# Compressing cached tokens: 32x32 blocks turned on VectorE, pages fetched over every second partition, direct products

## The chip, the cores and the metric

One NeuronCore of a Trainium2 chip runs the whole program once. The metric is the device time of that execution in microseconds. Everything is fp32.

## The reference, cut to what matters

The program is a four-layer decoder trunk that serves one prompt of 256 tokens and 8 sample sequences, each with 1024 cached tokens. Layers 0 and 3 use native sparse attention. One part of it compresses keys and values: each run of 32 tokens, taken every 16 tokens, is turned by a small two-layer network into one key and one value for each of the 4 KV heads.

```python
def _nsa_compress(kv_pad, cmp_pos, w1, w2):
    b, tpad = kv_pad.shape[:2]
    n_chunks = tpad // CMP_STRIDE                       # 64 for a sample, 16 for the prompt
    chunks = kv_pad[:, :, :2].reshape(b, n_chunks, CMP_STRIDE, 2, NSA_KV_HEADS, NSA_HEAD_DIM)
    w1 = w1.reshape(2, CMP_LEN, NSA_HEAD_DIM, CMP_HIDDEN)   # (2, 32, 64, 128)
    pos_bias = jnp.einsum('rld,rlde->re', cmp_pos, w1)
    pa = jnp.einsum('bnlrkd,rlde->bnrke', chunks, w1[:, :CMP_STRIDE])
    pb = jnp.einsum('bnlrkd,rlde->bnrke', chunks, w1[:, CMP_STRIDE:])
    hidden = jax.nn.gelu(pa[:, :-1] + pb[:, 1:] + pos_bias[:, None, :])
    out = jnp.einsum('bnrke,ref->bnrkf', hidden, w2)
    return out[:, :, 0], out[:, :, 1]
```

The cached tokens lie in pages of 128 tokens (`cache_nsa_kv`, 4 KB a token, of which the first 2 KB, the rows `r = 0, 1`, are compressed). Each sample has 8 pages, whose numbers come from `page_table`.

## The kernel before, in words

Each engine has one instruction list for each stage (`nc.Block`), and the engines meet at the end of a block. Within a block they wait for each other on semaphores. SP issues nearly all DMAs, in program order, among them the weights of all layers, which go through the four slots of `ring` (`issue`, lines 332 to 352).

The compression is `stage_nsa_compress` (lines 1226 to 1532). It runs twice, for layers 0 and 3. Its work is ordered as ten pairs `(g, r)`: `g` = 0 to 3 are groups of two samples (16 pages, 4 MB of used bytes), `g` = 4 is the prompt; `r` = 0 is for keys, `r` = 1 for values. Each pair `n` has four steps `j`, so there are 40 steps `m = 4 n + j`, of which the first 32 (`cached` = 8 pairs) belong to the samples.

- Pages. `chunk_pages` (line 940) fetches one group: for each page one DMA of 256 KB that puts half a chunk of 8 tokens into each of 16 partitions (`q:128:8` for page `q`). Group 0 is fetched in the stage before (`nsa_in_parts`, lines 1027 to 1032, where SP places these fetches between weight fetches; in layer 3, group 0 is fetched at line 1032 ahead of the last unit of weights). Group 1 is fetched at the start of the compression stage; groups 2 and 3 wait until the buffer (`G`, two of them) has been read (line 1317).
- Turning. TensorE transposes eight 128x128 blocks a step into PSUM (line 1353). VectorE (line 1479) and ScalarE (line 1498) each copy a half of the result into `x`.
- Products. The first-layer product of an even and an odd half chunk is split with differences of tokens: VectorE makes `before` (line 1458) and `after` (lines 1459 and 1460), and TensorE makes four products of 256 columns with them (lines 1391 and 1393) and two more (line 1401) with the sum of two weight blocks (`w_both`, line 1449). ScalarE copies the latter (line 1516), VectorE adds them (line 1467), and ScalarE applies gelu (line 1525).
- Second layer: `out(n)`, lines 1370 and 1376, one pair later.
- `weight_position` (line 1211) makes the position term on VectorE, 16 small instructions for each `r`.
- `w1` of 1 MB for `r` = 0 is fetched in the stage before (line 1024), for `r` = 1 at the start of the stage (line 1307), each by one DMA.
- At the end SP waits until the last cached product is made (line 1327) and issues 32 fetches of key pages (`key_pages`, line 932).

## Time and profile before

| | |
|---|---|
| time, median of 3 runs | 2560.42 us (2550.86 to 2567.43) |
| span of the profiled execution | 2552.3 us, from the first to the last instruction |
| TensorE busy | 2406.9 us, 94% of the span |
| VectorE / ScalarE busy | 1308.8 us (51%) / 735.5 us (29%) |
| DMA | 472.71 MB, mean 185 GB/s |
| compression stage, layer 0 | 159.7 to 309.4 us |
| compression stage, layer 3 | 1973.6 to 2125.2 us |

The time of a run is that of an execution by itself; the profiled one is told by its span, which is 8.1 us under the median. A busy time says how long an engine had an instruction under way. Matmuls overlap in TensorE, so the pitch from one to the next, read from their starts, is what counts, not the duration of one. Each fp32 product stands as two matmul instructions.

### The profile page before, as it was taken

What the parts mean: (1) busy time and instruction counts of PE and PEld (TensorE: products, weight loads), DVE (VectorE), ACT (ScalarE), POOL (GpSimd) and SP (SyncE); (2) the same over time, 40 slices, a digit from 0 to 9 for tenths busy, and PEclk for the clock granted to TensorE, in tenths of its full rate; (3) what the DMA queues carried; (4) which work ended last, traced back from release to release, by engine and by line L of the source; (5) the groups of instructions that cost most, each with busy time, mean ns of one, the idle gap of its engine ahead of it and who ended that gap; (6) DMA issues with size and microseconds to landing.
All of it is one profiled execution on the core that took longest, in us unless ns stands there. A gap on an engine that the chain in (4) does not pass through costs nothing. (4 is left out here: it accounts for less than half of the span.)

```text
span 2552.3 us, 45434 instructions
## 1 busy us (share of the span) xinstructions
PE 2406.9 (94%) x19182; PEld 2040.0 (80%) x19182; DVE 1308.8 (51%) x2332; ACT 735.5 (29%) x1763; POOL 26.4 (1%) x26
## 2 busy tenths in 40 slices
PE   8989988899999889999999898999999998979998
PEld 6668865699986767999888766899985786648998
DVE  2257384265552373666443285366631865535565
ACT  2125373221022342210232293221021445522200
POOL 0000000000000010000000010000000000000000
PEclk9999899999999979999999857999999997889999
DMA  9997616965644317666433255656671865293440
GB/s 346 307 241 166 210 49 214 350 229 213 245 160 144 99 56 283 212 251 223 154 132 134 68 150 195 233 204 256 217 207 66 181 177 159 71 321 122 172 170 22
DMA packets 287343, 472.71 MB, mean 185 GB/s; under 512 B 14956, under 2 KB 105149, under 8 KB 286662
## 3 DMA queue, kind: packets, MB, share of 16 engines
q1 hardware_dynamic: 272370, 456.04, 54.8%
q10 hardware_dynamic: 14770, 13.76, 1.7%
q8 instruction: 152, 2.49, 0.4%
q14 instruction: 51, 0.42, 0.1%
HBM read 448.72 MB, written 38.04 MB: 191 GB/s over the span
## 5 line engine op out<-in xcount | busy, mean ns | idle before, releaser
L631 PE MATMUL PS<-hT,ring 128*128 128x132 f32 x2048 | 249.7, 277 | 6.6 <-DVE hT L756 4.2
L631 PEld LDWEIGHTS PS<-hT,ring 128*128 128x128 f32 x2048 | 238.3, 190 | 11.9 <-issue 11.2
L631 PE MATMUL PS<-mT,arena 128*128 128x132 f32 x1536 | 184.6, 276 | 0.0
L631 PEld LDWEIGHTS PS<-mT,arena 128*128 128x128 f32 x1536 | 178.7, 190 | 0.0
L2687 PE MATMUL PS<-hT,ring 128*128 128x264 f32 x768 | 172.7, 386 | 0.1
L2687 PEld LDWEIGHTS PS<-hT,ring 128*128 128x128 f32 x768 | 145.1, 190 | 24.9 <-issue 0.4
L768 DVE TENSOR_TENSOR arena<-arena,PS 128x264 f32<-128x264 f32 x224 | 89.7, 427 | 130.8 <-PE PS L631 129.6
L715 ACT ACTIVATE arena<-arena 128x528 f32<-128x528 f32 x64 | 41.1, 642 | 312.1 <-DVE arena L768 312.1
L631 PE MATMUL PS<-arena,ring 128*128 128x132 f32 x1024 | 126.9, 277 | 0.0
L631 PE MATMUL PS<-hT,arena 128*128 128x132 f32 x1024 | 125.7, 276 | 0.0
L631 PE MATMUL PS<-mT,ring 128*128 128x132 f32 x1024 | 125.7, 276 | 0.0
L1479 DVE COPY arena<-PS 64x512 f32<-64x512 f32 (+1 forms) x160 | 94.1, 588 | 60.2 <-PE PS L1353 59.0
L631 PEld LDWEIGHTS PS<-arena,ring 128*128 128x128 f32 x1024 | 120.1, 190 | 2.4 <-issue 2.4
L631 PEld LDWEIGHTS PS<-hT,arena 128*128 128x128 f32 x1024 | 120.5, 190 | 0.3
L631 PEld LDWEIGHTS PS<-mT,ring 128*128 128x128 f32 x1024 | 120.2, 190 | 0.0
L1498 ACT ACTIVATE arena<-PS 64x512 f32<-64x512 f32 (+1 forms) x160 | 82.9, 518 | 121.1 <-PE PS L1353 120.0
L720 ACT ACTIVATE hT<-PS 128x264 f32<-128x264 f32 x8 | 3.1, 391 | 338.1 <-PE PS L631 338.1
L440 DVE TENSOR_SCALAR mT<-mT,coef_post 128x256 f32<-128x256 f32 x64 | 20.1, 351 | 154.2 <-ACT mT L394 154.1
L2115 PE MATMUL PS<-hT,ring 128*128 128x264 f32 x384 | 90.8, 392 | 4.9 <-PEq L1792 3.6
L2115 PEld LDWEIGHTS PS<-hT,ring 128*128 128x128 f32 x384 | 73.9, 193 | 18.2 <-issue 5.4
L2179 PE MATMUL PS<-hT,ring 128*128 128x264 f32 x384 | 85.9, 386 | 0.1
L1087 PE MATMUL PS<-ring,hT 128*128 128x512 f32 x192 | 84.7, 597 | 0.9 <-DMA ring<-in_nsa_w_in 0.9
(490 smaller groups left out, 4364.0 us busy)
## 6 DMA issues: line engine op xcount, KB each, us to landing
arena<-in_w_ada SPq DMA_DIRECT2D x36, 2048.0 KB, 12.1
ring<-in_w_mlp_in SPq DMA_DIRECT2D x32, 2048.0 KB, 8.7
ring<-in_w_mlp_out SPq DMA_DIRECT2D x32, 2048.0 KB, 8.1
ring<-in_w_ada SPq DMA_DIRECT2D x12, 2048.0 KB, 19.9
ring<-in_ssd_w_in SPq DMA_DIRECT2D x12, 2048.0 KB, 7.9
ring<-in_nsa_w_in SPq DMA_DIRECT2D x10, 2048.0 KB, 9.5
arena<-in_cache_nsa_kv SPq DMA_DIRECT2D x64, 256.0 KB, 10.5
ring<-in_cache_nsa_kv SPq DMA_DIRECT2D x64, 256.0 KB, 8.0
```

The source lines that it names most:

```text
L440: nc.vector.tensor_scalar_mul(mT[:, t, 0:SEQ], mT[:, t, 0:SEQ], coef_post[:, t, 0:1])
L631: ins = nc.tensor.matmul(PS[:, bank, at:at + HALF], lhs[:, k, p * 128:(p + 1) * 128], rhs[:, k, :], start=opens and k == 0, stop=closes an ...
L715: step(nc.scalar.activation(x, x, ACT.Relu))
L720: mlp_copied.on(nc.scalar.activation(n1, both(0), ACT.Copy))
L768: mlp_sums.on(nc.vector.tensor_tensor(dst, x, y, ALU.add))
L1087: ins = nc.tensor.matmul(PS[:, n % 4, :], hT[:, k, m * 128:(m + 1) * 128], w[:, k, :], start=k == 0, stop=k == 7)
L1479: ins = nc.vector.tensor_copy(dst, src)
L1498: ins = nc.scalar.activation(dst, src, ACT.Copy)
L2115: ins = nc.tensor.matmul(PS[:, 4 * h + m, 0:T], w[:, k, m * 128:(m + 1) * 128], src[:, 8 * d + k, :], start=d == 0 and k == 0, stop=d == d ...
L2179: ins = nc.tensor.matmul(PS[:, n % 4, 0:T], w[:, k, m * 128:(m + 1) * 128], hT[:, k, :], start=k == 0, stop=k == 7)
L2687: ins = nc.tensor.matmul(PS[:, n % 4, 0:T], w[:, k, m * 128:(m + 1) * 128], hT[:, k, :], start=k == 0, stop=k == 7)
```

## The change

The pages are fetched as two DMAs each: one for the even and one for the odd tokens of a page, 64 tokens each, one token (2 KB) into each second partition; sample `b` of the group has the partitions of parity `b`. A partition so holds 16 runs of 512 floats for a group. The source of such a DMA is walked as 4 (`i`, every 2 tokens) by 16 (`c`, every 8 tokens) runs; the destination is 64 partitions.

VectorE turns each step's tokens by one transpose instruction, which turns 32x32 blocks, straight from the page buffer into `x` (128 x 1024; 128 x 128 for the prompt). TensorE's transposes, the copies from PSUM on VectorE and ScalarE, the differences, the sum of weights, and the copy and addition of pairs are gone. TensorE makes eight products of 256 columns a step in place of six. The first-layer weights and the positions lie in another order, so `w1` is fetched by 16 DMAs of 32 partitions (128 runs of 512 B) and the positions by four.

```diff
--- before.py
+++ after.py
-        cmp_pos = par[:, 529:593].rearrange("p (l r j) -> p l r j", l=2, r=2)
+        cmp_pos = par[:, 529:593].rearrange("p (c l r h) -> p l r h c", c=4, l=2, r=2)
...
-        cache_chunks = a["cache_nsa_kv"].rearrange("l g (c t) r k d -> (l g) c t r (k d)", t=CMP // 2)
+        cache_quarters = a["cache_nsa_kv"].rearrange("l g (c i t) r k d -> (l g) t i c r (k d)", i=4, t=2)
...
-            slots = [ring[:, (st["used"] + 2 + i) % SLOTS, :, :] for i in range(2)]
-            return [[P(CMP // 2, 2 * KV * HD) for _ in range(2)], slots]
+            return [P(2 * PAGES, 2 * KV * HD), ring[:, 0:2].rearrange("p s k n -> p (s k) n")]
...
                     for q, number in zip(range(n, n + 4), numbers):
-                        page = cache_chunks[bass.ds(number + L * N_PHYS, 1), :, :, 0:2, :]
-                        fetched[g % 2].on(sp.dma_start(G[g % 2][b][q:128:PAGES],
-                                                       page.rearrange("g c t r n -> (g c) t (r n)")), 16)
+                        for t in range(2):
+                            part = cache_quarters[bass.ds(number + L * N_PHYS, 1), t, :, :, 0:2, :]
+                            fetched[g % 2].on(sp.dma_start(G[g % 2][b:128:2, 2 * q + t, :],
+                                                           part.rearrange("g i c r n -> (g i) c (r n)")), 16)
+
+        def compress_weights(sp, done, dst, L, r):
+
+            src = a["nsa_cmp_w1"][L, r].rearrange("(h i c d) e -> i d h c e", h=4, i=4, c=4)
+            to = dst.rearrange("p (h c e) -> p h c e", h=4, c=4)
+            for h in range(4):
+                for i in range(4):
+                    done.on(sp.dma_start(to[32 * i:32 * i + 32, h], src[i, :, h]), 16)
...
-                loaded2.on(sp.dma_start(mT_flat[:, 0:2048].rearrange("p (j e) -> p j e", j=16),
-                                        a["nsa_cmp_w1"][L, 0].rearrange("(j p) e -> p j e", p=128)), 16)
+                compress_weights(sp, loaded2, mT_flat[:, 0:2048], L, 0)
...
-                v.wait_ge(loaded2.sem, loaded2.at(16))
+                v.wait_ge(loaded2.sem, loaded2.at(256))
...
+            def rows_of(buffer, r, j):
+                return buffer.rearrange("p (y t) (r k h d) -> p t r h k y d", t=2, r=2, k=KV, h=2)[:, j // 2, r, j % 2]
+            def columns_of(j):
+                return x[:, j, :].rearrange("p (o b y) -> p y o b", o=4, b=2)
...
-                        sp.wait_ge(pt_ready.sem, pt_ready.at(8 * (g - 1)))
+                        sp.wait_ge(turned.sem, turned.at(8 * (g - 1)))
                         chunk_pages(sp, L, g, G)
                     sp.wait_ge(bias_near.sem, bias_near.at(32))
-                    sp.wait_ge(pt_ready.sem, pt_ready.at(24))
-                    src = kv_p[L, 0].rearrange("(c t) r k d -> c t (r k d)", t=CMP)[:, :, 0:512]
-                    for b in range(2):
-                        o = b * CMP // 2
-                        fetched[0].on(sp.dma_start(G[0][b][0:SEQ // CMP], src[:, o:o + CMP // 2]), 16)
+                    sp.wait_ge(turned.sem, turned.at(24))
+                    src = kv_p[L, 0].rearrange("(c i t) r k d -> i c t (r k d)", i=4, t=2)
+                    for i in range(4):
+                        fetched[0].on(sp.dma_start(G[0][32 * i:32 * i + 32, 0:2, :], src[i, :, :, 0:512]), 16)
...
-                    sp.wait_ge(mm_ready.sem, mm_ready.at(cached))
+                    sp.wait_ge(product_made.sem, product_made.at(4 * cached))
...
-                        o = PS[:, n % 2, :]
+                        o = product_bank(n)
+                        odd = x[:, j, 512:1024]
                         for u in range(2):
-                            nc.tensor.matmul(o[:, 0:256], w1[r][:, j + 4 * u, :], columns(whole(before[:, j, :]), u),
-                                             start=j == 0 and u == 0, stop=False)
-                            nc.tensor.matmul(o[:, 256:512], w1[r][:, 8 + j + 4 * u, :], columns(whole(after[:, j, :]), u),
-                                             start=False, stop=j == 3 and u == 1)
-                        if j == 0:
-                            if n < 2:
-                                pe.wait_ge(weights_summed.sem, weights_summed.at(n + 1))
-                            if n:
-                                pe.wait_ge(pairs_moved.sem, pairs_moved.at(n))
+                            first, second = w1[r][:, j + 4 * u, :], w1[r][:, 8 + j + 4 * u, :]
+                            at = 256 * u
+                            nc.tensor.matmul(o[:, 0:256], first, x[:, j, at:at + 256], start=j == 0 and u == 0, stop=False)
+                            nc.tensor.matmul(o[:, 256:512], first, odd[:, at:at + 256], start=False, stop=False)
+                            nc.tensor.matmul(o[:, 0:256], second, odd[:, at:at + 256], start=False, stop=False)
+                            ins = nc.tensor.matmul(o[:, 256:512], second, x[:, j, at + 1:at + 257], start=False,
+                                                   stop=j == 3 and u == 1)
...
-                    for j in range(4):
-                        turn(0, j)
-                    pe.wait_ge(loaded.sem, loaded.at(16))
                     for n in range(len(order)):
+                        if n == 1:
+                            pe.wait_ge(loaded.sem, loaded.at(256))
                         for j in range(4):
 
                             if n < cached:
-                                pe.wait_ge(differed.sem, differed.at(4 * n + j + 1))
-                                ins = cached_product(n, j)
+                                if n >= 2:
+                                    pe.wait_ge(given.sem, given.at(n - 1))
+                                pe.wait_ge(turned.sem, turned.at(4 * n + j + 1))
+                                product_made.on(cached_product(n, j))
                             else:
-                                pe.wait_ge(pt_taken.sem, pt_taken.at(4 * n + j + 1))
-                                pe.wait_ge(pt_taken2.sem, pt_taken2.at(4 * n + j + 1))
-                                ins = prompt_product(n, j)
-                            if j == 3:
-                                mm_ready.on(ins)
-                            if n + 1 < len(order):
-                                turn(n + 1, j)
+                                pe.wait_ge(turned.sem, turned.at(4 * n + j + 1))
+                                product_made.on(prompt_product(n, j))
...
+                    def turn(m):
+                        n, j = divmod(m, 4)
+                        g, r = order[n]
+                        if r == 0 and j == 0:
+                            loaded_group(v, g)
+                        if m >= 4:
+                            v.wait_ge(product_made.sem, product_made.at(m - 3))
+                        if n < cached:
+                            ins = nc.vector.transpose(columns_of(j), rows_of(G[g % 2], r, j))
+                        else:
+                            dst = x[:, j, 0:128].rearrange("p (u y q) -> p y q u", u=2, q=16)
+                            ins = nc.vector.transpose(dst, rows_of(G[g % 2], r, j)[:, :, 0, :])
+                        turned.on(ins)
...
                     v.wait_ge(loaded2.sem, loaded2.at(0))
-                    nc.vector.memset(after.rearrange("p j (x u q) -> p (j x) u q", u=2, q=8)[:, :, :, 7], 0.0)
-                    sum_weights(0)
+                    turn(0)
+                    turn(1)
                     position(0)
-                    for m in range(4 * len(order)):
+                    for m in range(1, last):
                         n, j = divmod(m, 4)
-                        if j == 3 and 0 < n <= cached:
-                            add_pairs(n - 1)
-                        v.wait_ge(pt_ready.sem, pt_ready.at(m + 1))
-                        for dst, src in regroup(m, 0):
-                            ins = nc.vector.tensor_copy(dst, src)
-                        pt_taken.on(ins)
-                        if n < cached:
-                            differences(m)
+                        if m + 1 < last:
+                            turn(m + 1)
+                        if m == 3:
+                            v.wait_ge(loaded.sem, loaded.at(256))
                         if 3 <= m < 7:
-                            if m == 3:
-                                v.wait_ge(loaded.sem, loaded.at(16))
-                                sum_weights(1)
                             for w in range(4 * (m - 3), 4 * (m - 2)):
                                 weight_position(v, w1[1], L, 1, w, cmp_weighted.at(w))
...
-                        regroups(4 * n + 6, 4 * n + 7)
-                        act.wait_ge(mm_ready.sem, mm_ready.at(n + 1))
-                        if n < cached:
-                            pairs_moved.on(nc.scalar.activation(pairs, PS[:, 2, 0:256], ACT.Copy))
-                        regroups(4 * n + 7, 4 * n + 8)
+                        act.wait_ge(product_made.sem, product_made.at(4 * n + 4))
                         if n < 2:
                             act.wait_ge(aux_taken.sem, aux_taken.at(n + 1))
                         if n < cached:
-                            act.wait_ge(sums_made.sem, sums_made.at(n + 1))
                             for e in range(2):
-                                dst = hid.rearrange("p (x q c e) -> p e x c q", x=8, q=8, e=2)[:, e]
-                                src = PS[:, n % 2, 256 * e:256 * e + 256].rearrange("p (x c q) -> p x c q", x=8, q=8)
+                                dst = hid.rearrange("p (y q e) -> p e y q", y=8, e=2)[:, e]
+                                src = product_bank(n)[:, 256 * e:256 * e + 256].rearrange("p (y q) -> p y q", y=8)
                                 ins = nc.scalar.activation(dst, src, ACT.Gelu_apprx_tanh, bias=p["pos"][:, r:r + 1])
...
+                    for c in range(4):
+                        dst = rows[16 * c:16 * c + 16, 5, :].rearrange("p (i d) -> p i d", i=4)
+                        tables_in.on(act.dma_start(dst, positions[c]), 16)
```

## Rows read from the trace of the kernel before

**Rows 1.** The page of the profiled execution, part 1: busy time of each engine.

```profile
PE 2406.9 (94%) x19182; PEld 2040.0 (80%) x19182; DVE 1308.8 (51%) x2332; ACT 735.5 (29%) x1763; POOL 26.4 (1%) x26
```

**Rows 2.** Windows of both compression stages: length, busy us of PE, PEld, DVE, ACT, POOL, then clock, DMA.

```profile
159.70:167.70 8.00, 5.85 (x35) 5.24 (x35) 7.49 (x15) 4.52 (x8) 0.00 (x0) 0.77 0.81 194
167.70:289.60 121.90, 119.21 (x723) 104.07 (x723) 91.98 (x181) 56.65 (x107) 0.00 (x0) 0.99 0.77 180
289.60:304.20 14.60, 14.60 (x119) 14.02 (x118) 2.79 (x11) 5.31 (x17) 0.00 (x0) 0.76 0.65 199
...
1981.60:2104.20 122.60, 117.66 (x723) 102.46 (x721) 92.71 (x183) 57.51 (x108) 0.00 (x0) 1.00 0.76 179
```

**Rows 3.** Timeline of TensorE, one step in the middle: start us, us, engine, line.

```profile
212.60 0.60 PE L1391 MATMUL PS<-ring,mT 128*128 128x256 f32 x2
...
214.33 1.03 PE L1401 MATMUL PS<-arena,ring 128*128 128x256 f32 x4
215.19 1.04 PE L1353 MATMUL PS<-wide,ring 128*128 128x128 f32 x8
216.06 0.60 PE L1391 MATMUL PS<-ring,hT 128*128 128x256 f32 x2
```

**Rows 4.** Waits of TensorE in the stage of layer 0: who for whom, us, times.

```profile
PE PS L1353 <- DMA ring<-in_cache_nsa_kv: 2.7, 1, 2.7
```

**Rows 5.** Timeline of SP's DMA issues, layer 0: start us, us until the last issue.

```profile
63.58 2.68 SPq L1024 DMA_DIRECT2D mT<-in_nsa_cmp_w  x1
67.25 10.72 SPq L948 DMA_DIRECT2D arena<-in_cache_nsa_kv  x8
78.02 2.45 SPq L351 DMA_DIRECT2D ring<-in_w_ada  x2
...
159.68 0.78 SPq L1307 DMA_DIRECT2D hT<-in_nsa_cmp_w  x1
...
163.60 12.39 SPq L948 DMA_DIRECT2D ring<-in_cache_nsa_kv  x16
...
289.60 19.35 SPq L932 DMA_DIRECT2D ring<-in_cache_nsa_kv  x32
309.36 0.39 SPq L1589 DMA_DIRECT2D arena<-bias_matrices  x1
```

**Rows 6.** Windows by DMA traffic: the last two numbers are the share of 16 engines and GB/s.

```profile
80.00:84.00 4.00, 4.00 (x11) 1.85 (x10) 3.61 (x12) 0.00 (x0) 0.00 (x0) 1.00 1.10 219
92.00:96.00 4.00, 4.00 (x11) 1.78 (x10) 0.00 (x0) 0.00 (x0) 0.00 (x0) 1.00 1.05 388
...
1399.50:1400.00 0.50, 0.50 (x4) 0.43 (x3) 0.00 (x0) 0.00 (x0) 0.00 (x0) 1.00 0.38 66
1415.50:1416.00 0.50, 0.50 (x4) 0.43 (x3) 0.00 (x0) 0.00 (x0) 0.00 (x0) 1.00 0.50 82
```

**Rows 7.** Groups of instructions in the stage of layer 0, VectorE: count, busy us, mean ns.

```profile
L1479 DVE COPY arena<-PS 64x512 f32<-64x512 f32 x64 | 43.6, 681 | 17.7 <-PE PS L1353 17.2
...
L1218 DVE SCALAR_TENSOR_TENSOR rstd<-hT,par,rstd 128x128 f32<-128x128 f32 x15 | 5.3, 351 | 0.4
...
L1449 DVE TENSOR_TENSOR ring<-mT 128x1024 f32<-128x1024 f32 x1 | 1.2, 1211 | 0.0
```

**Rows 8.** Timeline of TensorE at the first product of the stage of layer 0.

```profile
167.66 1.22 PE L1391 MATMUL PS<-ring,mT 128*128 128x256 f32 x2 [0.97 <-DMA hT<-in_nsa_cmp_w]
```

**Rows 9.** Timeline of TensorE in the stage before, layer 0.

```profile
86.38 0.33 PE L1053 MATMUL PS<-wide,ada_tmp 128*128 128x128 f32 x1 [0.23 <-DVE ada_tmp L1153]
...
103.73 7.13 PE L1087 MATMUL PS<-ring,hT 128*128 128x512 f32 x16 [0.92 <-DMA ring<-in_nsa_w_in]
```

**Rows 10.** Timeline of SP's DMA issues, layer 3.

```profile
1889.11 13.98 SPq L948 DMA_DIRECT2D arena<-in_cache_nsa_kv  x16
1903.15 0.57 SPq L351 DMA_DIRECT2D ring<-in_nsa_w_in  x1
```

**Rows 11.** Timeline of TensorE, layer 3: products with the last weight unit.

```profile
1946.88 14.00 PE L1087 MATMUL PS<-ring,hT 128*128 128x512 f32 x32
```

More of the change, by code:

```diff
@@ L1234, in stage_nsa_compress @@
             hid = P(512)
-            spare = [ring[:, (st["used"] + 4 + i) % SLOTS, :, :].rearrange("p k n -> p (k n)") for i in range(2)]
-            w_both = spare[0][:, 0:2048].rearrange("p (r j e) -> p r j e", r=2, j=8)
-            before = spare[1][:, 0:2048].rearrange("p (j n) -> p j n", j=4)
-            after = spare[1][:, 2048:4096].rearrange("p (j n) -> p j n", j=4)
-            pairs = p["vc_p"]
-            w1 = [x[:, 0:2048].rearrange("p (j e) -> p j e", j=16) for x in (mT_flat, hT_flat)]
+            w1 = [m[:, 0:2048].rearrange("p (j e) -> p j e", j=16) for m in (mT_flat, hT_flat)]
             w2 = ada_tmp[:, :].rearrange("p (r f) -> p r f", r=2)
@@ L1243, in stage_nsa_compress, with loaded_group, product_bank @@
             cached = 8
-            rows = lambda g: 128 if g < 4 else SEQ // CMP
-            fc = [0, 256, 256, 512, 288]
+            last = 4 * len(order)
+            def loaded_group(v, g):
+                v.wait_ge(fetched[g % 2].sem, fetched[g % 2].at((0, 512, 512, 1024, 512 + 64)[g]))
+            def product_bank(n):
+                return PS[:, n % 2, :]
             def compressed(act, n):
@@ L1336, in position @@
                         aux_ready.on(nc.tensor.matmul(PS[:, 3, r:r + 1], pos_terms[r], ones[:, 0:1], start=True, stop=True))
-                    def turn(n, j):
-                        m = 4 * n + j
-                        g, r = order[n]
-                        R = rows(g)
-                        if r == 0 and j == 0:
-                            pe.wait_ge(fetched[g % 2].sem, fetched[g % 2].at(fc[g]))
-                        if m >= 2:
-                            pe.wait_ge(pt_taken.sem, pt_taken.at(m - 1))
-                            pe.wait_ge(pt_taken2.sem, pt_taken2.at(m - 1))
-                        for b in range(2):
-                            for t in range(2):
-                                for at in range(2):
-                                    o = (2 * t + at) * 128
-                                    c = r * 256 + at * 128
-                                    ins = nc.tensor.transpose(PS[:, 4 + 2 * (m % 2) + b, o:o + R],
-                                                              G[g % 2][b][0:R, 2 * j + t, c:c + 128], ident[0:R, 0:R])
-                        pt_ready.on(ins)
                     def out(n):
@@ L1376, in out @@
                                     ins = nc.tensor.matmul(PS[0:63, 3, (i * 4 + k) * 64:(i * 4 + k + 1) * 64],
-                                                           h[:, k // 2, k % 2, i, 0:N_CMP_S], w2[:, 1, :], start=True, stop=True)
+                                                           h[:, i, k, 0:N_CMP_S], w2[:, 1, :], start=True, stop=True)
                         else:
@@ L1407, in prompt_product @@
                         r = order[n][1]
-                        for b in range(2):
+                        for u in range(2):
                             for h in range(2):
-                                ins = nc.tensor.matmul(PS[:, n % 2, 0:KV * N_CMP_P], w1[r][:, 8 * h + j + 4 * b, :],
-                                                       prompt_columns(j, b)[:, :, h:h + N_CMP_P],
-                                                       start=j == 0 and b == 0 and h == 0, stop=j == 3 and b == 1 and h == 1)
+                                ins = nc.tensor.matmul(PS[:, n % 2, 0:KV * N_CMP_P], w1[r][:, 8 * h + j + 4 * u, :],
+                                                       prompt_columns(j, u)[:, :, h:h + N_CMP_P],
+                                                       start=j == 0 and u == 0 and h == 0, stop=j == 3 and u == 1 and h == 1)
                         return ins
@@ L1463, in add_pairs @@
-                    def add_pairs(n):
-                        v.wait_ge(pairs_moved.sem, pairs_moved.at(n + 1))
-                        o = PS[:, n % 2, :].rearrange("p (a n) -> p a n", a=2)
-                        sums_made.on(nc.vector.tensor_tensor(o, o, bc(pairs, 1, 2), ALU.add))
+                    def turn(m):
[11 more added lines that the diff above has]
+                        turned.on(ins)
```

69 lines of the change are left out of this document (12 added, 57 removed).

## The prediction

> **What bounds the kernel now.** I read the page first: TensorE is busy for 94% of the span and no other engine comes near [rows 1]. The change touches the two compression stages, so I took windows of those [rows 2]. From 167.7 to 289.6 us, the 32 cached steps, TensorE is busy 119.2 of 121.9 us at full clock, while VectorE has 92.0 us of work and ScalarE 56.7. So TensorE bounds this stretch. Its timeline shows one step: the first product starts at 212.60, the pair products at 214.33, the transposes at 215.19, and the next step at 216.06 [rows 3]. That is 3.46 us, of which the twelve matmul instructions (six products of 256 columns) take 215.19 - 212.60 = 2.59, or 0.216 each, and the eight transposes 0.87. TensorE waits for pages once, 2.7 us [rows 4].
>
> What ends the stage is another thing. SP starts the 32 key fetches when the last cached product is made, at 289.60; they take it 19.4 us to issue, and it comes to the next stage's first DMA at 309.36 [rows 5]. The prompt steps on TensorE take 14.6 us to 304.2 [rows 2]. SP leaves the block last, so the stage lasts from 159.68 to 309.36 [rows 5], and its length is the time of the 32nd cached step plus 19.8 us. Work saved in the prompt steps is worth nothing.
>
> **TensorE's work.** Removed are eight transposes a step, 0.87 us, and four matmul instructions of pairs, 4 x 0.216 = 0.86. Added are eight: the new step has eight products, 16 x 0.216 = 3.46 us. The old one took 3.46. So TensorE gains nothing in the bound stretch; the words "all products direct" buy back just what the transposes free. In the prompt steps the small transposes go, but there SP ends the stage.
>
> **VectorE and ScalarE.** A step's two copies of 64x512 and three differences give way to one transpose instruction of 128x1024. No row shows one. I take 1.2 us, the 128x1024 addition of line 1449, which has its shape. From below I bound it by 0.7, one copy of 512 elements a partition at 0.681; from above by 2.7, twice the 1.36 that 1024 elements cost at the copies' rate, since writing in single scattered elements may be slower [rows 7]. All are under 3.46, so TensorE hides them; VectorE would decide only beyond that. TensorE now waits for the turn (`turned`) and VectorE for the product four steps back, which leaves three steps, 10.4 us, of room. The sum of pairs and ScalarE's copies were off the path. At the start a gain: the first product came 8.0 us after the stage began, held last by the 1 MB of w1 for values [rows 5, 8]; now it needs one turn and comes at about 2 us, and w1 is needed four products later, at 2 + 13.9 = 16 us. Behind that wait stand VectorE's 16 position instructions, 16 x 0.35 = 5.6 us [rows 7], for which TensorE then stands about 3 us. So +3 of the 6 is spent again.
>
> **SP's issues.** A page's fetch takes SP 12.39/16 = 0.77 us, a key page's 19.35/32 = 0.60 [rows 5]. A group had 16 and has 32 of them: between 19 and 25 us. w1 was one DMA of 0.78 us and is 16, at 0.39 (a plain fetch) to 0.77 each [rows 5]: 6 to 12 us. I take 8.5, between the two. They stand before the pages of group 1, so those start not 3.9 us into the stage (163.60 - 159.68) but at 3.9 - 0.8 + 8.5 = 11.6.
>
> **The pages' transfers.** This decides. While old page fetches run alone the 16 DMA engines are all busy, 1.10, but move 219 GB/s; weights move 388 GB/s at 1.05, with runs of 2 KB in both [rows 6]. The old fetch writes 16 partitions, 8 apart. A spread of partitions can so halve the rate, and the new one, 64 partitions of one parity, may lift that. But the rows have a second way to lose. Two small stores (3 rows and then 8 rows of 8 KB, each row one piece) run with no more than 0.50 and 0.38 of the engines busy [rows 6], where everything that is cut in 16 or 128 rows outermost reaches 1.0. A transfer seems to be dealt to no more engines than its outermost dimension has entries. The new fetch has 64 partitions on its SBUF side, but its DRAM side is walked as 4 runs (`i`) of 16 (`c`), and `i` is outermost: the old one had 16 (`c`) outermost on both sides. If the smaller side counts, each page runs on 4 engines, at 4/16 of 388 = 97 GB/s; if the larger, on 16 and up to 388. All narrow transfers in the trace have the same number on both sides, so no row tells which. I take 4, since a deal of runs to engines must split both sides alike.
>
> The Trainium skill says this outright: "DMA: Bandwidth & Descriptors", section "Why a DMA increments its semaphore by 16 and not by 1", has a transfer from SP run on the largest number of engines, up to 16, that divides the outermost sizes of both sides; for 4 and 64 that is 4. The trace agrees as far as it goes, 0.50 for 8 rows. It says for gain in "SBUF - State Buffer", section "Door 1: The DMA port swizzle", that partitions reach 16 ports by bits 2 to 4 and 6 of their number; the old fetch's partitions reach 8 of them, the new one's all 16. The halved rate of the old pages, 219 against 388, agrees. By that rule alone the pages would get faster; by the first they get slower.
>
> **Sum for 4 engines.** A group is 32 x 128 KB = 4.19 MB, 43.2 us at 97 GB/s, against 29 us for eight steps and two `out`. So the pages bound the stage. Three groups queue behind each other (the waits `turned` for 8 and 16 pass before SP comes to them): 11.6 + 3 x 43.2 = 141, +2 for the bias tables between them, +2 for landing: 145 us. Then one turn, 1.2, eight steps, 27.7, two `out`, 2.1, and some 3 us of a lower clock after an idle stretch (the first window of the stage ran at 0.77 [rows 2]): the 32nd step ends at 179. With SP's 19.8 the stage is 199 us, where it was 149.7: +49. For layer 3 the old stretch is 0.7 us longer [rows 2]: +48. Together +97.
>
> Before the stage. In layer 0 the weights queue behind group 0's pages with no room: the third projection unit arrived 0.9 us late at 103.73 [rows 9]. Half a group, 2.1 MB, now holds the four engines 21.6 us where it took 10 (67.25 to 78 [rows 5]): +11, and w1's 16 issues add about 3 there, for TensorE also waited, 0.23 us, on VectorE at 86.38, which stood behind w1 [rows 9]: +14. The second half meets the last modulation weights, whose slack is unknown: 0 to 12, I take 5. In layer 3 the pages were issued from 1889.11 and the last weight unit at 1903.15 [rows 10]; pages now last until about 1897 + 43 = 1940, the unit lands near 1949, and its use began at 1946.88 [rows 11]: +2. Together +21. The three more position fetches at the start are off the path or under 1.5 us.
>
> Sum: 97 + 21 = 118 on the span of 2552.3, or 2670; the median of the runs is 8.1 above that span, so 2678, rounded to 2675.
>
> **Rivals.**
> A, on the other side: the fetches run on all 16 engines. Then a group needs 11 us at 388 GB/s, and SP's issue is what delays it. Group 1's last page is issued at 11.6 + 19 to 25 = 31 to 37 us and lands by 33 to 42; its step is due at 2 + 27.7 + 1 + 3 = 34. So 0 to 8 us of waiting, mid 5; groups 2 and 3 come in time. The 32 steps with their `out` take 118.3 without waits (121.9 less the 2.7 of pages and 0.9 of a slow start; 32 x 3.46 = 110.8 of it, the rest seven `out` of 1.1) [rows 2, 4]. The 32nd ends at 2 + 118.3 + 3 + 5 = 128, against 129.9 now. The stage is 2 us shorter, twice; before it VectorE's wait on w1 costs about 3 and shorter page traffic gives up to 5. Result 2556, range 2535 to 2580. It decides if the larger side's count rules. For it: VectorE's spare time and the doubled rate. Against: the rows of narrow transfers.
> B: VectorE becomes the bound. A turn that takes T > 3.46 us costs 32 x (T - 3.46) in each stage; at T = 4.5 that is +66 in all under A (2622), and nothing under the forecast while T stays under 5.4, where pages still bound. Against it: no 128x1024 instruction of VectorE in these stages is over 1.22 us.
> C: as forecast, but four engines alone run faster than a sixteenth each of 388, as nothing crowds them. At a tenth more, 107 GB/s, each stage is 12 us shorter (2651), and with the weights' slack absorbing most of the 21 us before it, it is 2635. That is the low end of the forecast.
>
> **How the numbers follow.** Forecast (pages on 4 engines) 0.72; A 0.22; B 0.06. The forecast's own range is 2630 to 2715: below by C, above by a rate a tenth lower (+28) and the larger weight delays. To leave out no more than 2 in 10 the range must take in A's centre: 2545 to 2715. A measurement of this kernel tells about 1% from no change, 26 us. Faster by over 1% (under 2535): only A's edge, 0.06. Within 1%: most of A, 0.19. Slower: the forecast, B and A's rest, 0.75.
>
> **What would show it.** In the changed profile: DMA share near 0.25 and about 100 GB/s while pages alone are fetched, in windows of the stage; TensorE or VectorE waiting for DMA of pages about 14 us before each of groups 2 and 3, more before 1; the step still at 3.46 us; the turn near 1.2 us; stage lengths near 199 us; the third projection unit of layer 0 late by over 10 us. If the share is near 1 and the rate near 388, A holds, and the forecast is wrong by its main term. If the step isn't 3.46, the term of TensorE is wrong; if VectorE's turn is over 3.46, B holds.

## The result, and the profile after

The changed kernel takes 2681.69 us, the median of four runs (2677.99 to 2687.43), against 2561.28 for the one before in the same comparison (2550.86 to 2567.43). The ratio is 1.0477, with a 95% interval of 1.044 to 1.0513: the change makes the kernel 120 us slower. The span of the profiled execution is 2679.4 us, 127.1 more than before.

The page of the changed kernel, part 1, answers to [rows 1]:

```profile
PE 2413.4 (90%) x18798; PEld 2033.6 (76%) x18798; DVE 1240.9 (46%) x2038; ACT 640.8 (24%) x1587; POOL 26.4 (1%) x26
```

TensorE has nearly the same work; VectorE has 68 and ScalarE 95 us less. What was longer was the waiting. The first view for that is the timeline of SP's DMA issues in layer 0, changed kernel, which answers to [rows 5] (start us, us until the last issue):

```profile
64.07 9.90 SPq L957 DMA_DIRECT2D mT<-in_nsa_cmp_w  x16
74.73 14.62 SPq L948 DMA_DIRECT2D arena<-in_cache_nsa_kv  x16
...
191.16 7.48 SPq L957 DMA_DIRECT2D hT<-in_nsa_cmp_w  x16
...
199.83 34.85 SPq L948 DMA_DIRECT2D ring<-in_cache_nsa_kv  x32
...
238.10 41.47 SPq L948 DMA_DIRECT2D arena<-in_cache_nsa_kv  x32
280.60 40.53 SPq L948 DMA_DIRECT2D ring<-in_cache_nsa_kv  x32
...
367.86 18.96 SPq L932 DMA_DIRECT2D ring<-in_cache_nsa_kv  x32
387.23 0.39 SPq L1518 DMA_DIRECT2D arena<-bias_matrices  x1
```

The compression stage now lasts from 191.16 to 387.23, or 196.1 us, where it took 149.7. The 32 fetches of group 1 fill 34.9 us of SP's line, those of groups 2 and 3 fill 41: 1.1 and 1.3 us for each, where one of the old took 0.77. The same 32 issues take 24.65 us where only the walk of the source is another (the version with 16 runs, below), so SP is held back here by the transfers. The windows by DMA traffic of the changed kernel show them (length, busy us of PE, PEld, DVE, ACT, POOL, then clock, share of 16 engines, GB/s; as [rows 6]):

```profile
205.00:225.00 20.00, 12.47 (x58) 10.40 (x57) 7.74 (x15) 2.15 (x3) 0.00 (x0) 0.86 0.26 100
...
290.00:315.00 25.00, 23.62 (x112) 20.19 (x112) 14.38 (x8) 2.29 (x5) 0.00 (x0) 0.93 0.27 102
```

The share of 0.26 is what 4 of the 16 engines give when they are always busy, and they move 100 GB/s: a quarter of the 388 that all sixteen moved for weights [rows 6]. In the timeline of VectorE, same stage, the turns that had to wait for pages stand where each group has landed:

```profile
245.12 3.65 DVE L1413 STREAM_TRANSPOSE arena<-ring 128x1024 f32<-128x1024 f32 x2 [31.65 <-DMA ring<-in_cache_nsa_kv]
...
289.31 7.21 DVE L1413 STREAM_TRANSPOSE arena<-arena 128x1024 f32<-128x1024 f32 x4 [13.28 <-DMA arena<-in_cache_nsa_kv]
...
333.46 7.21 DVE L1413 STREAM_TRANSPOSE arena<-ring 128x1024 f32<-128x1024 f32 x4 [23.16 <-DMA ring<-in_cache_nsa_kv]
```

From one to the next are 44.2 and 44.2 us: a group of 4.19 MB at 95 GB/s. The groups queue behind each other, and the stage follows them. TensorE's waits over the whole of layer 0's attention input and compression (60 to 400 us, changed kernel: who for whom, us, times, longest) are these:

```profile
PE PS L1334 <- DVE arena L1401: 31.5, 1, 31.5
...
PE PS L370 <- DMA ring<-in_w_ada: 18.8, 2, 12.0
PE PS L1358 <- DVE arena L1413: 16.9, 3, 12.6
...
PE PS L1538 <- PEq L1288: 10.1, 1, 10.1
...
PE PS L1094 <- DMA ring<-in_nsa_w_in: 7.2, 1, 7.2
```

The first and the third are the pages of groups 1, 2 and 3, seen through VectorE. The second and the last are weights that queue behind the pages of group 0 in the stage before. The fourth is the end of the compression stage: all engines stand while SP issues the key fetches, the last computing instruction being ScalarE's at 377.22, ten microseconds before SP leaves.

The added 127.1 us lie so: 31.5 before the first stage (191.16 less 159.68), 46.4 in it, 1.0 between the stages (layer 3's begins at 2052.59, before at 1973.69), 49.8 in the second (2052.59 to 2253.92, 201.3 against 151.5), and 1.6 less behind it. What lies before a stage moves from one execution to the next. Four of the versions below, those with one transfer a page and SP's order as it was up to there, have the same code before the first stage, which begins at 168.44, 169.15, 177.90 and 182.19 us in their profiled runs. So the 31.5 us are well clear of that, but a difference of under 14 us there, read from one pair of executions, is not.

### The profile page after: what moved, and what is told of

Read it like the earlier page. It is cut to its first block and busy times, and to the rows that moved or that the text cites. A ratio compares the mean times of both kernels' runs of the same rounds, so it can differ in the third digit from the quotient of the medians.

```text
span 2679.4 us, 44539 instructions
## 1 busy us (share of the span) xinstructions
PE 2413.4 (90%) x18798; PEld 2033.6 (76%) x18798; DVE 1240.9 (46%) x2038; ACT 640.8 (24%) x1587; POOL 26.4 (1%) x26
## 5 line engine op out<-in xcount | busy, mean ns | idle before, releaser
L631 PEld LDWEIGHTS PS<-hT,ring 128*128 128x128 f32 x2048 | 238.3, 190 | 12.0 <-issue 11.3
L2616 PEld LDWEIGHTS PS<-hT,ring 128*128 128x128 f32 x768 | 145.1, 190 | 24.9 <-issue 0.4
L1413 DVE STREAM_TRANSPOSE arena<-ring 128x1024 f32<-128x1024 f32 x32 | 60.9, 1941 | 158.3 <-DMA ring<-in_cache_nsa_kv 113.5
L2044 PEld LDWEIGHTS PS<-hT,ring 128*128 128x128 f32 x384 | 74.9, 196 | 18.7 <-issue 5.4
L2108 PEld LDWEIGHTS PS<-hT,ring 128*128 128x128 f32 x384 | 72.8, 190 | 13.0 <-issue 0.6
```

Source lines behind the costliest of these rows:

```text
L631: ins = nc.tensor.matmul(PS[:, bank, at:at + HALF], lhs[:, k, p * 128:(p + 1) * 128], rhs[:, k, :], start=opens and k == 0, stop=closes an ...
L1413: ins = nc.vector.transpose(columns_of(j), rows_of(G[g % 2], r, j))
L2044: ins = nc.tensor.matmul(PS[:, 4 * h + m, 0:T], w[:, k, m * 128:(m + 1) * 128], src[:, 8 * d + k, :], start=d == 0 and k == 0, stop=d == d ...
L2108: ins = nc.tensor.matmul(PS[:, n % 4, 0:T], w[:, k, m * 128:(m + 1) * 128], hT[:, k, :], start=k == 0, stop=k == 7)
L2616: ins = nc.tensor.matmul(PS[:, n % 4, 0:T], w[:, k, m * 128:(m + 1) * 128], hT[:, k, :], start=k == 0, stop=k == 7)
```

## The experiments

**The number of runs that is walked outermost.** If the deal of a transfer to engines causes the loss, only the way in which the same bytes are walked need change. The source's outermost size 4 becomes 16, 8 or 2, by one number in the line; bytes, destination, number of transfers and every instruction that computes stay. The tokens land in another order, so these versions compress other values.

```diff
-        cache_quarters = a["cache_nsa_kv"].rearrange("l g (c i t) r k d -> (l g) t i c r (k d)", i=4, t=2)
+        cache_quarters = a["cache_nsa_kv"].rearrange("l g (c i t) r k d -> (l g) t i c r (k d)", i=16, t=2)
```

> The changed kernel, but each half page's source is walked as 16 runs of 4 in place of 4 runs of 16; the same bytes go to the same 64 partitions, in another order, so the compressed keys and values are not the reference's. Theory (a page is dealt to as many engines as the smaller outermost size): 16 engines, pages at over 300 GB/s, stage about 149 us in place of 196, the 31 us before the first stage back but for 3; about 2556 us. Rival (two DMAs a page, or partitions of one parity, are slow in themselves): stays at 2680.

> As walk16, with 8 runs of 8; the same part is not the reference's. Theory: 8 engines, DMA share near 0.5 and about 195 GB/s while pages alone move; a group takes 21.6 us, less than its eight steps, so about 2560 us. Rival: stays at 2680.

> As walk16, with 2 runs of 32; the same part is not the reference's. Theory: 2 engines, share 0.13, 50 GB/s; a group takes 84 us in place of 42, so each stage is 3 x 42 = 126 us longer and the stages before them some 40 and 35 us: about 3010 us. Rival: stays at 2680.

Measured: 16 runs give 2577.45 us, ratio 1.007 (1.0048 to 1.0093), so 104 of the 120 us are gone. 8 runs give 2590.42 (one run), 30 over their expectation; 2 runs give 3016.3 (one run), as expected. The window by DMA traffic while pages alone are fetched, 2 runs outermost (columns as above):

```profile
260.00:300.00 40.00, 0.21 (x1) 0.00 (x0) 0.00 (x0) 0.00 (x0) 0.00 (x0) 0.56 0.13 51
```

The same view with 8 runs outermost:

```profile
180.00:200.00 20.00, 12.69 (x60) 10.60 (x58) 7.97 (x15) 2.15 (x3) 0.00 (x0) 0.92 0.43 142
```

And with 16:

```profile
176.00:200.00 24.00, 17.37 (x81) 14.72 (x79) 12.27 (x20) 2.15 (x3) 0.00 (x0) 0.90 0.55 162
```

The shares are 0.13, 0.26 (changed kernel), 0.43 and 0.55. The first two are what 2 and 4 of 16 engines give when they are always busy, though the other side of the transfer has 64 partitions in each. So a small outermost size on the source limits the engines, however large that of the destination is, and that is shown. In every version the source has the smaller size; that a small size on the destination does the same, no run shows. With 8 runs the share stays a little under 0.5, and SP takes 29.15 us for 32 fetches, so the expected 195 GB/s are not reached. With 16 runs the share no longer shows the limit of the engines but SP's pace: it issues a group's 32 fetches in 24.65 us, 0.77 each, as it issued the old ones, and 4.19 MB in that time are 170 GB/s. The expected 300 GB/s could not be reached so.

With 16 runs the kernel was to take 2556 (rival A) and took 2577. TensorE's waits in its stage of layer 0 show what rival A had left out, here the first of them:

```profile
PE PS L1334 <- DVE arena L1401: 12.9, 1, 12.9
```

and the same wait in the timeline of TensorE:

```profile
206.31 1.11 PE L1334 MATMUL PS<-arena,ada_tmp 128*64 128x126 f32 x8 [12.94 <-DVE arena L1401]
```

Line 1401 is the 0.15 us copy of the position term for values. VectorE makes it in step 8, behind `turn(8)` and `turn(9)`, whose tokens are the first of group 1. `out(0)` waits for this copy itself (`aux_taken` at 2), since its result goes to the place in PSUM from which the term is copied (`PS[:, 3]`), and TensorE has `out(0)` ahead of two further steps of group 0. So TensorE stands with work of group 0 in hand for pages of group 1. The stage lasts 158.9 us where rival A had about 148; 8 of these 11 are this wait beyond the 5 that were allowed, and the rest isn't broken down. Before the stage it is 7.4 us longer; TensorE waits 5.4 us there for a projection unit, where it had waited 0.9 [rows 9].

**How much of the loss is group 0's.** Only the pages of group 0, which are fetched in the stage before, are walked as 16 runs.

```diff
-                            part = cache_quarters[bass.ds(...
+                            part = (cache_wide if g == 0 else cache_quarters)[bass.ds(...
```

> The changed kernel with only group 0's pages walked as 16 runs of 4 (those are the pages that are fetched in the stages before the compression stages); group 0's compressed tokens are not the reference's. Theory: takes away the loss before the stages and nothing in them: 31.5 less 3 us in layer 0 and about 1 in layer 3, so 2682 - 29 = 2653 us, with both compression stages at 196 us.

Measured: 2649.18, ratio 1.0362 (1.0318 to 1.0406), 32.5 us less than the changed kernel, where 29 were expected. The first compression stage begins 23.8 us earlier (167.40, not 191.16) and is as long as in the changed kernel (195.7); layer 3's begins 32.2 us earlier (2020.36, not 2052.59). Of these 8 further us the pages ahead of layer 3 can have made only 1.4: from SP's first fetch of w1 there to the stage it is 84.8 us, not 86.2 (1935.53 and 1966.36 to the stage), and 6.7 lie before that, where the two kernels are the same. Group 0's share is so the 23.8 us before the first stage (28.5 were expected) and next to nothing in layer 3; the rest of the loss is made by groups 1 to 3.

**The old kernel with the new walk.** The rival cause is that something other than the walk came with the change: two transfers a page, every second partition, or VectorE's turn. So the kernel before gets only the other order of runs; its half chunks then hold other tokens.

```diff
-        cache_chunks = a["cache_nsa_kv"].rearrange("l g (c t) r k d -> (l g) c t r (k d)", t=CMP // 2)
+        cache_chunks = a["cache_nsa_kv"].rearrange("l g (t c) r k d -> (l g) c t r (k d)", c=4)
```

> The kernel before, with nothing changed but the order in which a page's source is walked: 4 runs outermost of 32 tokens each, where it was 16 of 8; the same bytes, the same 16 partitions, the same number of DMAs, and the compressed keys and values are not the reference's. Theory (the smaller outermost size deals the transfer to 4 engines): 100 GB/s or less, 42 us a group, so each stage is bound by pages and ends near 3.9 + 3 x 42 + 4 + 2 + 30 + 20 = 186 us in place of 150; with some 20 us before the first one about 2650 us. Rival (the loss came from the rest of the change): no difference to before, 2560.

Measured: 2704.17, ratio 1.0583 (1.0545 to 1.062), the slowest but for the two-run walk. Its window by DMA traffic in the stage of layer 0:

```profile
250.00:280.00 30.00, 24.79 (x143) 21.81 (x144) 16.93 (x32) 11.36 (x21) 0.00 (x0) 0.83 0.26 99
```

and SP's issues there:

```profile
207.83 35.00 SPq L948 DMA_DIRECT2D ring<-in_cache_nsa_kv  x16
...
247.30 40.73 SPq L948 DMA_DIRECT2D arena<-in_cache_nsa_kv  x16
289.06 40.52 SPq L948 DMA_DIRECT2D ring<-in_cache_nsa_kv  x16
```

Same share, same rate, same 40 us a group with 16 issues as with 32: neither the number of transfers nor the partitions nor the turn is needed for the loss. The mechanism was as expected, the size was not (54 us more). The stages came to 204.2 and 207.0, not 186. TensorE's timeline of the first shows why:

```profile
344.94 1.97 PE L1353 MATMUL PS<-wide,ring 128*128 128x128 f32 x8 [13.02 <-DMA ring<-in_cache_nsa_kv]
```

Group 3 is there 141.0 us into the stage (136 expected), and the last cached product ends 43.4 us later (388.35), where 30 were expected. The old kernel's TensorE transposes one pair ahead: `turn(6, 0)`, which waits for group 3, stands behind the first of four products of pair 5. So 11 steps follow the arrival there, and 8 in the changed kernel. Before the first stage it is 44.3 us more, not 20: TensorE waits 28.2 us there for weights, and 5.6 us lie ahead of the first page fetch (72.81, not 67.25), where the two kernels are the same; the rest isn't broken down.

**One transfer a page, 8 runs outermost.** The same tokens as in the changed kernel reach every product, by more engines: one DMA of 256 KB for each page, over all 128 partitions, walked 8 (`i`) by 16 (`c`).

```diff
-                        for t in range(2):
-                            part = cache_quarters[bass.ds(number + L * N_PHYS, 1), t, :, :, 0:2, :]
-                            fetched[g % 2].on(sp.dma_start(G[g % 2][b:128:2, 2 * q + t, :],
-                                                           part.rearrange("g i c r n -> (g i) c (r n)")), 16)
+                        page = cache_pairs[bass.ds(number + L * N_PHYS, 1), :, :, 0:2, :]
+                        fetched[g % 2].on(sp.dma_start(G[g % 2][:, PAGES * b + q, :],
+                                                       page.rearrange("g i c r n -> (g i) c (r n)")), 16)
```

The turns go by sample and half in place of step, so a step's product needs two of them.

> The changed kernel with one DMA a page, walked as 8 runs of 16 into all 128 partitions; the token's parity lies in the partition and the sample in the columns, and VectorE's turns are arranged so that the result is that of the reference. Theory: 8 engines, 195 GB/s, 21.6 us a group, half the issues of SP; the stages at about 149 us and 2553 us in all, equal to the kernel before or 5 to 10 us under it. Rival (16 engines' worth is needed): over 2600.

Measured: 2593.08, ratio 1.0142 (1.0116 to 1.0168), 40 over the expectation. The stages last 164.1 and 165.1 us, not 149. Windows of it, the first stage, while groups 1, 2 and 3 come in:

```profile
180.00:190.00 10.00, 10.00 (x48) 8.79 (x47) 7.86 (x11) 1.67 (x2) 0.00 (x0) 1.00 0.53 145
...
205.00:215.00 10.00, 1.36 (x9) 1.06 (x10) 3.64 (x3) 0.21 (x1) 0.00 (x0) 0.50 0.54 155
...
248.00:264.00 16.00, 16.00 (x86) 13.84 (x85) 8.38 (x5) 2.30 (x5) 0.00 (x0) 1.00 0.53 203
```

The share is that of 8 engines, as 8 runs should give. But for group 1 and most of group 2 they move 145 to 155 GB/s, and only for group 3 the expected 195 and more. A group at the lower rate takes some 28 us instead of 21.6. And TensorE's waits there have the wait that the walk by 16 had shown:

```profile
PE PS L1343 <- DVE arena L1410: 15.0, 1, 15.0
PE PS L1367 <- DVE arena L1423: 3.3, 1, 3.3
```

**Is VectorE's turn hidden?** In that version each cached turn is made twice, so VectorE has 32 turns more in each stage.

```diff
+                            stepper(v, dve_step)(nc.vector.transpose(pair_columns(h, b), pages_of(G[g % 2], r, h, b)))
                             ins = nc.vector.transpose(pair_columns(h, b), pages_of(G[g % 2], r, h, b))
```

> one_page8 with each cached turn done twice on VectorE, one after the other. The turn takes 1.94 us. Theory (TensorE's 3.46 us a step hides the turn): twice 1.94 and a wait is 3.9 to 4.0 us a step, over 3.46, so VectorE now bounds: 32 x 0.5 = 16 us more in each stage, about 2585 us. If a second turn cost its full 1.94 a step, the turn wasn't hidden: 32 x 1.94 x 2 = 124 us more.

Measured: 2620.19, ratio 1.0242 (1.0207 to 1.0276), 27 us over the version with single turns. In VectorE's timeline of the first stage, where it makes turn after turn, a pair of turns comes every 3.80 us:

```profile
267.47 1.92 DVE L1423 STREAM_TRANSPOSE arena<-arena 128x1024 f32<-128x1024 f32 x1
...
271.27 1.97 DVE L1423 STREAM_TRANSPOSE arena<-arena 128x1024 f32<-128x1024 f32 x1
```

That is 0.34 more than TensorE's step of 3.46, and for 32 steps 11 us. The spans of the two profiled runs differ by 32.6 us: the stages are 11.1 and 10.8 us longer (175.3 and 176.0), and 9.5 us lie before the first (177.90, not 168.44), where the two kernels are the same. So the turns cost about 22 us, where 32 were expected. Of the 124 us of added work (64 x 1.94) about four fifths is hidden. So rival B's mechanism is there, over 3.46 us a step, where the prediction had put it; a single turn of 1.94 lies far under it.

**Where the position copy stands.** It goes ahead of the turn that waits for pages, in the changed kernel and in the one-page version.

```diff
+                        if m == 7:
+                            position(1)
                         if m + 1 < last:
                             turn(m + 1)
...
-                        if m == 8:
-                            position(1)
```

> The changed kernel with VectorE's copy of the second position term moved ahead of the turn that waits for group 1's pages; before, the output of the first pair on TensorE, and the two steps behind it, stood behind that wait. Theory (with 4 engines the arrival of group 3 ends the 32nd step): no change, 2682 us, though TensorE makes two more steps before the first long wait. Rival (the wait behind the position term counts in the end): 2 x 7 = 14 us less, 2668.

> The same move in one_page8, where pages land faster than TensorE's steps use them once group 1 is in. Theory: TensorE gains the two steps that it stood idle before, 2 x 6.9 = 14 us less than one_page8, 2579. Rival (group 1's arrival isn't the only thing late): under 5 us less.

Measured: nothing in the changed kernel (2681.49; 1.0475, 1.0437 to 1.0513), and 20 us in the one-page version (2573.0; 1.0059, 1.0035 to 1.0084). In the changed kernel TensorE's wait in the stage of layer 0 only changes its name; it is 46.6 us where the two were 31.5 + 16.9:

```profile
PE PS L1358 <- DVE arena L1413: 46.6, 4, 22.8
```

In the one-page version it shrinks from 15.0 + 3.3 to 10.6:

```profile
PE PS L1367 <- DVE arena L1423: 10.6, 2, 7.5
```

The two stages of its profiled run are 7.3 and 8.2 us shorter, near the 14 expected; the rest of the 20 isn't in them. That is the same edit where pages bound the stage and where they nearly don't.

**The key fetches at the end.** In the one-page version the keys that go to ring slots already free are fetched before the last cached product.

```diff
-                    sp.wait_ge(product_made.sem, product_made.at(4 * cached))
-                    key_pages(sp, l, 2)
-                    key_pages(sp, l, 3)
+                    if l:
+                        key_pages(sp, l, 2)
+                        key_pages(sp, l, 3)
+                    else:
+                        key_pages(sp, l, 3)
+                        sp.wait_ge(product_made.sem, product_made.at(4 * cached))
+                        key_pages(sp, l, 2)
```

> one_page8 with the key fetches of the ring slots that the stage doesn't use issued before the last cached product: half of them in layer 0, all in layer 3. Theory (SP's 19.4 us of key issues end the stage): in layer 0 the stage ends 9.4 us sooner, at the 32nd step plus 10, where TensorE's prompt steps end also (9.4 us after it in the changed kernel); in layer 3 at about the 32nd step plus 10 too: 2 x 9 = 18 us less than one_page8, about 2535 us. Rival (the prompt steps on TensorE end it): no change.

Measured: 2568.59, ratio 1.004 (1.0023 to 1.0057), 24 us less than the one-page version, where 18 were expected; the 2535 expected stood on a one-page version of 2553. The stages last 151.8 and 152.8 us, 12.3 less each, which is the whole gain. So the stage's end is SP's, as the trace of before had shown [rows 5].

**All together.** One transfer a page, the position copy and the keys early, and `w1` for values issued on ScalarE's queue; then also `w1` for keys.

```diff
-                    compress_weights(sp, loaded, hT_flat[:, 0:2048], L, 1)
...
                 def _(act):
+                    compress_weights(act, loaded, hT_flat[:, 0:2048], L, 1)
```

> one_page8 with the position copy moved, the early key fetches, and the 16 fetches of w1 for values issued by ScalarE's queue instead of SP's, so that group 1's pages start 7.5 us sooner. Theory: 2593 - 24 (early keys, as measured) - 14 (position) - 15 (w1 off SP, twice 7.5) = 2540, 0.7% under the kernel before. Rival (the pages' own 27 us a group is then the bound): 2550 to 2560.

> combined, and w1 for keys too is issued by ScalarE's queue, in the stage before. Theory (SP's 10 us of issues there delay the weight stream of layer 0): 5 to 9 us less than combined. Rival (the 1 MB itself or its 512 B runs delay the stream, whoever issues it, or ScalarE's copies come late behind the issues): no change or a few us more.

Measured: 2547.89, ratio 0.9962 (0.994 to 0.9984), and 2545.0, ratio 0.9933 (0.991 to 0.9956). Both beat both kernels, by little; the first is 8 us over its expectation and 2 under its rival's range. Its stages last 141.6 and 143.6 us, 8 less than in the kernel before, and its first one begins 10.7 later. No run gives the kernel before the early keys, which took 24 us from the one-page version. So it isn't shown that the turns on VectorE and the direct products have a part in this gain. The second step was to bring 5 to 9 us and brought 2.9, which the overlap of the two intervals doesn't separate from nothing. In TensorE's waits of the first (58 to 320 us), below, its target is the first line; in the second that line is gone, while the wait for modulation weights is 4.5 us instead of 3.1:

```profile
PE PS L1093 <- DMA ring<-in_nsa_w_in: 6.5, 1, 6.5
...
PE PS L370 <- DMA ring<-in_w_ada: 3.1, 1, 3.1
```

A version that walks by 16 runs and still puts each token where the products need it, as with four transfers a page, was not tried.

## Why the prediction was right

It said 2675 and the time is 2682. By its steps:

- **Four engines.** Right, and shown by the walks of 2, 8 and 16 and by the old kernel with four runs. The forecast had 97 GB/s and 43.2 us a group; 95 and 44.2 were measured. The rule that the prediction took from the Trainium skill ("DMA: Bandwidth & Descriptors", section "Why a DMA increments its semaphore by 16 and not by 1") agrees with shares of 0.13 for 2 against 64 and 0.26 for 4 against 64; sizes that don't divide each other, and a smaller one on the destination, no run has. The rule on partitions and ports was not put to a test: the changed kernel's pages moved 25 GB/s for each of four engines, and with 16 runs SP's issue set the pace. Of the prediction's reason, that a deal must split both sides alike, the runs show only the case of a small source.
- **TensorE's step.** Right. In the changed kernel's timeline a step begins at 255.33 and the next at 258.79, 3.46 us as before [rows 3]. The first product starts at 193.25, 2.1 us into the stage, as forecast.
- **The stage.** 196.1 us where 199 was forecast: group 3 arrives 142.3 us into it (145), the 32nd step ends at 176.7 (179), and SP takes 19.4 more. It starts the pages at 8.7 rather than 11.6, since `w1` takes 7.5 us and one small fetch of 0.43 stands besides. The added time of both stages is 96.2; the forecast was 97. (Its +48 for layer 3 took the old stage there for 0.7 us longer; it is 1.8, so its own terms give +47.)
- **VectorE's turn.** Mis-sized: 1.94 us, not 1.2, inside the bounds of 0.7 and 2.7. Off the path, as the doubled turns showed.
- **Before the stage.** Mis-sized, the largest error: 31.5 us, not 19, in layer 0. The delays were estimated for the third projection unit, 14, and for the second half, 5. Measured are 6.8 us of TensorE waiting for modulation weights at 108.05, 7.2 for the projection unit at 118.89 and 12.0 for modulation weights again at 174.84, or 26.0, and TensorE works more slowly after the waits, at a granted clock of 0.50 (1.2 GHz) from 104 to 122 us, where before it had 1.00 (2.4 GHz) from 103 to 112. 64 matmul instructions of modulation take 3.64 us there and 1.93 to 1.96 in most other places, the sixteen of the projection 9.63 and 7.13. That is 2 x 1.7 + 2.5 = 5.9, and with the waits 31.9, of which 1.1 was there before [rows 9]. The last delay had been given "0 to 12, I take 5"; it was at the upper end. In layer 3, 1.0 and 2 forecast.
- **The waits for groups 2 and 3.** Half right. TensorE was to wait about 14 us for each. For group 3 it waits 12.6; for group 2 only 2.75, because out(0) and two steps of group 0 were pushed behind group 1's arrival and fill the gap. VectorE, with nothing of the kind to do, waits 13.3 and 23.2.
- **The missed wait.** The prediction had TensorE standing 3 us for the position term and didn't look at what stands ahead of the copy on VectorE. It costs nothing while pages bound the stage (the copy moved: 2681.49), but rival A's 2556 was 21 us short, by it and by what wasn't broken down.
- **The offset.** The median was to stand 8.1 us over the span; it stands 2.3 over. With a span 9.4 longer than the forecast's 2670, the two misses cancel in part, and 2678 was rounded down to 2675. That the total is 7 off is in part luck; the four engines and the length of the stage are not.
- **Rivals.** A and B are excluded: A by the share of 0.26, B by the turn of 1.94 us and its doubling. C, faster engines, too: while pages alone are fetched no window of 5 us moves over 104 GB/s, and a group takes longer than forecast, not less.

## What to carry to other kernels

Read both sides of a transfer before changing its pattern. Here a source walked by 2 or 4 runs outermost kept 2 or 4 engines at work, with the same bytes, and with 16 or 64 partitions on the other side. When a product is made direct to save work, count that work where the stage is bound; here it saved VectorE and ScalarE 163 us together and the path nothing, and what was won back in the end came from page fetches on eight engines, from SP's order and from one small copy that stood behind a wait for pages. A cheap instruction on an in-order engine can hold others as long as the longest wait ahead of it: moving this one gave nothing where pages bound the stage, and 7 to 8 us a stage where they nearly didn't.

## What the runs showed of the hardware

- Two engines moved 51 GB/s and four 100, or 25 each. Eight (share 0.53) moved 145 to 155 GB/s in some stretches, or 18 to 19 each, and 198 to 203, or 25 each, in others. The same fetches of group 3, into the same buffer, have the higher rate in the one-page version (203, above) and the lower one in the version with all edits together, whose group 2 has the higher:

```profile
205.00:222.00 17.00, 17.00 (x95) 14.63 (x92) 9.97 (x6) 3.53 (x8) 0.00 (x0) 1.00 0.53 198
238.00:258.00 20.00, 20.00 (x105) 17.36 (x104) 8.54 (x6) 3.02 (x7) 0.00 (x0) 1.00 0.53 143
```

  So neither the destination nor the walk sets the lower rate. What does isn't settled.
- The transposition of 128x1024 fp32 values in blocks of 32x32 takes VectorE 1.94 us, from either page buffer, and that of 128x128 0.41. The groups of VectorE in the changed kernel's stage of layer 0:

```profile
L1413 DVE STREAM_TRANSPOSE arena<-ring 128x1024 f32<-128x1024 f32 x16 | 30.5, 1941 | 76.3 <-DMA ring<-in_cache_nsa_kv 54.8 <-PE PS L1361 21.5
...
L1416 DVE STREAM_TRANSPOSE arena<-arena 128x128 f32<-128x128 f32 x6 | 2.4, 406 | 12.3 <-PE PS L1361 11.4 <-PE PS L1370 0.9
```

- SP's issue line is no measure of SP's own cost when the engines are slow: the same page fetch takes 0.77 us of it with 16 runs outermost and 1.1 to 1.3 with four. A plain fetch of 32 partitions takes 0.47 (7.48 us for 16).
- TensorE comes back from a long wait at half its clock: after the 31.5 us wait products of 256 columns start 0.85 us apart (250.99, 251.84) and a few products later 0.43 (254.04, 254.47). The granted clock was 0.50 (1.2 GHz) in the one stretch and 0.98 (2.4 GHz nearly throughout) in the next:

```profile
249.00:253.50 4.50, 4.50 (x16) 3.52 (x17) 0.00 (x0) 1.21 (x3) 0.00 (x0) 0.50 0.28 103
253.50:258.00 4.50, 4.50 (x22) 3.92 (x21) 1.96 (x1) 0.00 (x0) 0.00 (x0) 0.98 0.26 99
```

  The slower start cost some 2 us here, and 5.9 us behind the three waits before the stage.
